# The down projection of a two-layer transformer trunk as seven block products in place of eight, each part right behind its up part

## The chip, the cores and the metric

The kernel runs on one core of a Trainium2 chip. The core has five engines that work side by side and meet by semaphores: TensorE (PE in the rows) multiplies matrices from SBUF into PSUM, VectorE (DVE) and ScalarE (ACT) do elementwise work, GpSimd (POOL) does elementwise work on SBUF alone, and SyncE (SP) issues the DMA transfers. The metric is the device time of one execution in microseconds; lower is better.

## The reference

Two layers, each for a prompt of 512 positions and a sample of 32 (together T = 544 columns, kept feature-major: features on the 128 partitions, positions along the free axis). The changed part is the feed-forward network of a layer:

```
u = rmsnorm(x) @ w_up                       # 1024 -> 2 * 2816
uc = conv_b + causal depthwise conv of width 3 over positions
gate, val = uc[..., :D_FF], uc[..., D_FF:]
f = (jax.nn.gelu(gate, approximate=True) * val) @ w_down      # 2816 -> 1024
x = x + rmsnorm(f, g_post_ffn)
```

Around it stand two attention branches and a per-layer embedding, which the change does not touch.

## The kernel before

**Precision.** A float32 product is made of three passes of a rounded type. Weight and activation are split into a high part (the value rounded) and a low part (value minus high), and `PARTS` runs high*high, high*low, low*high into the same PSUM bank. So each weight chunk needs one rounding and one subtraction (both on POOL), and each activation tile one rounding (ACT) and one subtraction (DVE, helper `lo`, L1099 to L1103).

**Weights.** They come through a ring of four slots in SBUF (`SLOTS`). SP loads chunk after chunk in the order of `STREAM` as soon as TensorE is done with the chunk four places ahead; POOL then rounds it (L616) and writes the low part in place over the loaded values (L623). A chunk is 128 x 1024 (`upg`, `upv` and most `down` chunks), 128 x 768 for the down chunks of the last part.

**The feed-forward part.** Its 2816 hidden features are 22 tiles of 128, in three parts of 8, 8 and 6 tiles (`FFN_PARTS`). An up tile takes two chunks, gate (`upg`) and value (`upv`), each of 8 x 3 x 2 = 48 matmuls of 272 columns. A down chunk `("down", i, j)` multiplies part i's tiles into output tile j of 8: 48 matmuls (36 in the last part), two column halves of 272 in two banks. The order on TensorE is up 0, up 1, down 0, up 2, down 1, down 2, so each down part has another part's work between it and its inputs (`g_s` has two buffers).

**What follows a chunk.** When TensorE is done with an up chunk, DVE scales the result out of PSUM (`u_tile`, L1462 to L1464), ACT starts the convolution (L986 to L995, `conv0`), DVE adds the two other taps (L1470, L1472); after the value chunk DVE multiplies gelu and value into `gt` (L1494, L1495), ACT rounds `gt` (`g_high`, L1007) and DVE makes the low part (`g_low`, through L1101). For the next tile DVE does `u_tile` again first and then the low part. A down result is copied by ACT (down 0, L1023) or added by DVE (down 1 and 2, L1509) into `fT`.

**PSUM.** Banks 4 to 7 hold the convolution; the results of matmuls go in turn into bank pairs (0, 1) and (2, 3). A list of events gives each result tile its banks at build time, and `banks_free` makes TensorE wait until the last user of a bank has been read.

## Time and profile before

| | us |
|---|---|
| median of 3 runs (lowest, highest) | 1851.71 (1851.10, 1852.47) |
| the profiled execution's own time | 1849.15 |
| its span, first to last instruction | 1847.4 |
| TensorE busy | 1824.8 (99%) |
| VectorE busy | 923.5 (50%) |
| ScalarE busy | 559.5 (30%) |
| GpSimd busy | 1075.4 (58%) |

The profile is of one execution. Busy times overlap, since the engines work side by side; their shares say how full an engine is over the whole span and nothing of a single stretch. The profiled execution took 1.75 us more than its span, and the median of the runs is 4.3 us above that span.

### The profile page before, as it was taken

Reading aid. Unit: us, or ns where it says so; the run is one execution under the profiler, and the core shown is the slowest. Engines: PE = TensorE matmul, PEld = TensorE weight load, DVE = VectorE, ACT = ScalarE, POOL = GpSimd, SP = SyncE. Lnnn points to the kernel's source line nnn. Section 1 sums busy time; section 2 is a strip of 40 time slices with the busy share of each in tenths; the row PEclk is TensorE's granted clock in tenths of the full one; section 3 lists DMA queues with packets and bytes.
Section 4 is the critical chain, followed back from the end, with each engine's and each line's share of the span. In section 5 each row is a group of like instructions: output and inputs, shape, how many; then the busy total and the mean of one; then the engine's idle time right before and its main releaser. Section 6 shows DMA issues by size and latency. Waiting matters only on the chain.

```text
span 1847.4 us, 33704 instructions
## 1 busy us (share of the span) xinstructions
PE 1824.8 (99%) x14214; PEld 1768.4 (96%) x14214; DVE 923.5 (50%) x1634; ACT 559.5 (30%) x1197; POOL 1075.4 (58%) x996
## 2 busy tenths in 40 slices
PE   9999999999999999999999999999999999999999
PEld 8999889999999999999999998899999999999999
DVE  6666775232755532523556767752336555235143
ACT  4444443112422211202344445430133222112021
POOL 8686534656555555557665864446456555555564
PEclk9999999999999999999999999999999999999999
DMA  5242112233222222223343421222422222222222
GB/s 189 88 132 86 54 42 84 88 120 112 72 90 92 84 89 92 86 80 97 99 143 93 127 87 47 70 66 84 152 81 75 86 92 89 84 92 91 79 86 95
DMA packets 76231, 170.49 MB, mean 92 GB/s; under 512 B 6384, under 2 KB 34160, under 8 KB 76080
## 3 DMA queue, kind: packets, MB, share of 16 engines
q1 hardware_dynamic: 68752, 160.79, 27.1%
q10 hardware_dynamic: 7328, 7.54, 1.2%
q8 instruction: 113, 1.85, 0.4%
q14 instruction: 38, 0.31, 0.1%
HBM read 156.41 MB, written 9.79 MB: 90 GB/s over the span
## 4 chain that ended last, share of the span: by engine, by line
PE 92%; DVE 5%; ACT 1%; POOL 1%; issue 1%; DMA 0%; SPq 0%; DVEq 0%; ACTq 0%; POOLq 0%
PE ps L1579 76%; PE ps L1614 3%; PE ps L1742 2%; PE ps L1700 2%; DVE xn L1101 1%; DVE xT L1446 1%; DVE mix L1443 1%; PE ps L1796 1%; PE ps L1653 1%; PE ps L1802 1%; DVE R L1101 1%; PE ps L1719 1%; DVE xT L1264 1%; PE ps L1668 1%; PE ps L1738 1%
## 5 line engine op out<-in xcount | busy, mean ns | idle before, releaser
L1579 PE MATMUL ps<-xn,wsp 128*128 128x272 f32 x7824 | 1002.0, 289 | 5.7 <-issue 2.2
L1579 PEld LDWEIGHTS ps<-xn,wsp 128*128 128x128 f32 x7824 | 986.1, 189 | 10.8 <-issue 6.0
L616 POOL CAST wsp<-raw 128x1024 fp32r<-128x1024 f32 (+2 forms) x222 | 220.1, 997 | 505.0 <-DMA raw<-in_wstream 450.3
L623 POOL TENSOR_TENSOR wsp<-raw,wsp 128x1024 fp32r<-128x1024 f32 (+2 forms) x278 | 492.1, 1782 | 16.2
L1579 PE MATMUL ps<-R,wsp 128*128 128x272 f32 x3840 | 486.2, 288 | 0.1
L1579 PEld LDWEIGHTS ps<-R,wsp 128*128 128x128 f32 x3840 | 482.7, 188 | 1.2 <-DVE xT L1130 0.5
L610 POOL TENSOR_TENSOR wsp<-raw,wsp 128x256 fp32r<-128x256 f32 x304 | 235.5, 795 | 12.2
L605 POOL CAST wsp<-raw 128x512 fp32r<-128x512 f32 x152 | 112.2, 738 | 147.9 <-DMA raw<-in_wstream 113.3
L1101 DVE SCALAR_TENSOR_TENSOR R<-ps,R 64x256 fp32r<-64x256 f32 (+12 forms) x264 | 130.0, 510 | 73.2 <-ACT R L753 24.6
L1462 DVE TENSOR_TENSOR mix<-ps,rstd 128x272 f32<-128x272 f32 x88 | 38.8, 441 | 202.9 <-PE ps L1579 192.6
L986 ACT ACTIVATE mix<-vv 128x2 f32<-128x2 f32 x88 | 17.9, 204 | 363.0 <-DVE mix L1464 363.0
L1101 DVE SCALAR_TENSOR_TENSOR R<-mix,R 128x544 fp32r<-128x544 f32 (+2 forms) x86 | 73.2, 852 | 81.1 <-ACT R L1007 66.9
L1470 DVE SCALAR_TENSOR_TENSOR ps<-mix,vv,ps 128x546 f32<-128x546 f32 x88 | 69.4, 789 | 55.6 <-ACT ps L995 55.6
L1614 PE MATMUL ps<-xn,wsp 128*128 128x272 f32 x576 | 80.3, 294 | 6.7 <-DVE xn L1101 6.7
L1614 PEld LDWEIGHTS ps<-xn,wsp 128*128 128x128 f32 x576 | 74.5, 188 | 10.7 <-DVE xn L1101 9.7
L1509 DVE TENSOR_TENSOR A<-ps,A 128x544 f32<-128x544 f32 x32 | 23.2, 724 | 110.1 <-PE ps L1579 110.1
L1264 DVE TENSOR_TENSOR_SCAN xT<-xT 128x128 f32<-128x128 f32 (+3 forms) x64 | 62.9, 1024 | 19.2 <-ACT xT L843 19.2
L995 ACT ACTIVATE ps<-mix,vv 128x546 f32<-128x546 f32 x88 | 71.4, 812 | 1.6 <-DVE mix L1464 1.6
L1472 DVE SCALAR_TENSOR_TENSOR ps<-mix,vv,ps 128x546 f32<-128x546 f32 x88 | 69.6, 791 | 3.1
L1115 DVE TENSOR_TENSOR acc<-acc,mix 128x544 f32<-128x544 f32 x30 | 30.8, 1027 | 64.6 <-ACT mix L666 64.6
L666 ACT ACTIVATE mix<-A 128x544 f32<-128x544 f32 x16 | 10.6, 661 | 150.4 <-DVE A L1509 150.4
L1742 PE MATMUL ps<-R 128*128 128x512 f32 x192 | 52.4, 408 | 0.0
(230 smaller groups left out, 1529.2 us busy)
## 6 DMA issues: line engine op xcount, KB each, us to landing
raw<-in_wstream SPq DMA_DIRECT2D x233, 512.0 KB, 3.5
raw<-in_wstream SPq DMA_DIRECT2D x48, 128.0 KB, 2.6
raw<-in_wstream SPq DMA_DIRECT2D x16, 384.0 KB, 3.0
raw<-in_kc SPq DMA_DIRECT2D x8, 512.0 KB, 3.8
raw<-in_vc SPq DMA_DIRECT2D x8, 512.0 KB, 4.8
xT<-in_x_in SPq DMA_DIRECT2D x8, 272.0 KB, 5.3
out_k_out<-mix ACTq DMA_DIRECT2D x8, 272.0 KB, 2.9
xT<-in_x_in SPq DMA_DIRECT2D x1, 2176.0 KB, 9.2
```

Of the source, the lines that this page charges most:

```text
L605: nc.gpsimd.tensor_copy(dst[:, 0, f], part[:, f]).then_inc(S["w_hi"], 1)
L610: ins = nc.gpsimd.tensor_tensor(dst[:, 1, f], part[:, f], dst[:, 0, f].bitcast(F32), ALU.subtract)
L616: ins = nc.gpsimd.tensor_copy(dst[:, 0, f], part[:, f])
L623: ins = nc.gpsimd.tensor_tensor(dst[:, 1, f], part[:, f], dst[:, 0, f].bitcast(F32), ALU.subtract)
L995: ac(uc[v], e[:, 0:T + 2], ACT.Identity, scale=vv[:, V_CW + f:V_CW + f + 1], bias=vv[:, V_CB + f:V_CB + f + 1]).then_inc(S["conv0"], 1)
L1101: ins = v.scalar_tensor_tensor(dst, src, scale, hi.bitcast(F32), ALU.mult, ALU.subtract)
L1264: v.tensor_tensor_scan(x, x, x, 1.0, ALU.mult, ALU.min).then_inc(S["r_done"], 1)
L1470: link(v.scalar_tensor_tensor(uc[w], uext[w][:, 1:T + 3], vv[:, V_CW + 2 * FT + f:V_CW + 2 * FT + f + 1], uc[w], ALU.mult, ALU.add))
L1472: v.scalar_tensor_tensor(uc[w], uext[w][:, 2:T + 4], vv[:, V_CW + 4 * FT + f:V_CW + 4 * FT + f + 1], uc[w], ALU.mult, ALU.add).then_inc(S[ ...
L1579: mm = pe.matmul(z[:, h], w[:, x, (k0 + k) * P:(k0 + k + 1) * P], rhs[:, y, k, h * HT:(h + 1) * HT], start=(k == 0 and (x, y) == (0, 0)), ...
L1614: mm = pe.matmul(z[:, h], w[:, x, k * P:(k + 1) * P], xn[:, y, k, h * HT:(h + 1) * HT], start=(k == 0 and (x, y) == (0, 0)), stop=(k == KT ...
L1742: mm = pe.matmul(z.rearrange("p r (b q) -> p r b q", b=2), val[:, x, kb], a[:, :, :, kb * P:(kb + 1) * P], start=(kb == 0 and i == 0), sto ...
```

## The change

The eight output tiles of the down projection are taken in pairs (j, j+4), the tiles of a part in two halves of h = 4, 4 and 3, and the 544 columns in two halves of 272 (`HT`). Each pair is then a product of 2 x 2 blocks: weights A11, A12, A21, A22 and activations B11, B12, B21, B22. Strassen's scheme (in Winograd's form) makes it of seven products P1 to P7 of h x 3 matmuls each, on sums of blocks:

- of weights, on DVE (`weight_sum`): S1 = A21 + A22, S2 = S1 - A11, S3 = A11 - A21, S4 = A12 - S2; each is 128 x 512 (384 in the last part) and is rounded by ACT (`sum_high`), its low part made by POOL;
- of activations, on DVE in `product`: T1 to T4 from the halves of `gt`, each 128 x 272, rounded by ACT and split by DVE (`g_low`, `lows_left`);
- of results: P6 goes on top of P1 in its bank and P7 on top of that; ACT copies the bank at each stage into the bank of P2, P3 and P4 (`hand_on`), on which these accumulate; DVE collects into `fT`.

The order is now up 0, down 0, up 1, down 1, up 2, down 2. The sums have one buffer each, so a sum of the next pair waits for the product that reads the present one. The diff, cut to its core:

```diff
-FFN = _up(0) + _up(1) + _down(0) + _up(2) + _down(1) + _down(2)
+    return [("down", i, j + n) for j in range(NP) for n in (0, NP)]
+FFN = _up(0) + _down(0) + _up(1) + _down(1) + _up(2) + _down(2)
+DOWN_LOWS = ("A11", "S1", "S3", "A22", "S2", "A12", "S4")
...
+            if kind == "turn":
+                ring = freed + [4, 5, 6, 7]
+                continue
+            if kind == "lend":
+                BANKS[t] = (ring[0],)
...
+            if c[0] == "down":
+                return ("P2", c[1], c[2]) if c[2] < NP else ("P4", c[1], c[2] - NP)
...
+        DOWN_BY = {"P1": "A11", "P2": "A12", "P3": "S4", "P4": "A22", "P5": "S1", "P6": "S2", "P7": "S3"}
...
@@ gpsimd
+                            if ch[2] < NP:
+                                nc.gpsimd.tensor_copy(dst[:, 0, 0:w], part).then_inc(S["w_hi"], 1)
+                                highs += 1
+                                continue
+                            nc.gpsimd.tensor_copy(hi["A22"], whole_sum["A22"]).then_inc(S["w_hi"], 1)
+                            highs += 1
+                            pool.wait_ge(S["w_hi"], highs)
+                            for n in DOWN_LOWS:
+                                if n in SUMS:
+                                    pool.wait_ge(pre["sum_hi"], sums_made(layer, i, j, n))
+                                pool.wait_ge(pre["sum_raw"], sums_made(layer, i, j, {"A11": "S3", "S1": "S2", "S3": "S3", "A22": "S1"}.get(n, "S4")))
+                                nc.gpsimd.tensor_tensor(lo[n], whole_sum[n], hi[n].bitcast(F32), ALU.subtract).then_inc(S["w_lo"], 1)
...
@@ scalar
+                        for j in range(_F0[i], _F0[i + 1]):
+                            if j == end:
+                                for n in ("S1", "S2", "S3"):
+                                    sum_high(i, 0, n)
+                            u_tile(("upg", j))
+                            if j == end:
+                                sum_high(i, 0, "S4")
+                            u_tile(("upv", j))
+                            if j == end:
+                                hand_on(i, 0, "P1", "P2")
+                            act.wait_ge(S["conv2"], 2 * j + 1)
+                            ac(gel, uc[0], ACT.Gelu_apprx_tanh).then_inc(S["gelu_done"], 1)
+                            g_high(j, (lambda: hand_on(i, 0, "P6", "P3")) if j == end else None)
+                        for j in range(NP):
+                            if j > 0:
+                                hand_on(i, j, "P1", "P2")
+                            if j < NP - 1:
+                                sum_high(i, j + 1, "S1")
+                            if j > 0:
+                                hand_on(i, j, "P6", "P3")
+                            if j < NP - 1:
+                                sum_high(i, j + 1, "S2")
+                                sum_high(i, j + 1, "S3")
+                            hand_on(i, j, "P7", "P4")
+                            if j < NP - 1:
+                                sum_high(i, j + 1, "S4")
...
@@ vector
+                    def product(j):
...
+                        if first:
+                            v.scalar_tensor_tensor(g_raw[:, 1, kk, G_T2], gt[:, HT:T], 1.0, gt[:, 0:HT],
+                                                   ALU.mult, ALU.subtract).then_inc(S["g_raw"], 1)
+                            g_low(j, G_B11, gt[:, 0:HT])
+                            g_low(j, G_T1, g_raw[:, 1, kk, G_T2])
+                            return
+                        v.scalar_tensor_tensor(g_raw[:, 1, kk, G_T4], gt[:, HT:T], 1.0, g_raw[:, 1, kk, G_T2],
+                                               ALU.mult, ALU.subtract).then_inc(S["g_raw"], 1)
+                        g_low(j, G_B21, gt[:, 0:HT])
+                        g_low(j, G_T2, g_raw[:, 1, kk, G_T4])
+                        v.scalar_tensor_tensor(g_raw[:, 1, kk, G_T3], gt[:, HT:T], 1.0, g_raw[:, 1, kk, G_T3],
+                                               ALU.mult, ALU.subtract).then_inc(S["g_raw"], 1)
+                        dve.wait_ge(S["g_lo"], G_LO[j, G_T2])
+                        v.scalar_tensor_tensor(g_raw[:, 1, kk, G_T4], gt[:, 0:HT], 1.0, g_raw[:, 1, kk, G_T4],
+                                               ALU.mult, ALU.subtract).then_inc(S["g_raw"], 1)
...
+                            if j == end:
+                                for n in ("S1", "S2", "S3"):
+                                    weight_sum(i, 0, n)
+                            if j != 1:
+                                u_tile(("upg", j))
+                            if j == end:
+                                weight_sum(i, 0, "S4")
+                            if j > _F0[i]:
+                                lows_left(j - 1, (G_B22, G_T3))
+                            taps(("upg", j))
+                            u_tile(("upv", j))
...
+                            if j > _F0[i]:
+                                lows_left(j - 1, (G_T4,))
+                            taps(("upv", j))
+                            product(j)
+                        lows_left(end, (G_B22, G_T3, G_T4))
+                        for j in range(NP):
...
+                            collect(i, "P5", j, ((j + NP, 1), (j, 1)), True)
+                            if j < NP - 1:
+                                for n in ("S1", "S2", "S3"):
+                                    weight_sum(i, j + 1, n)
+                            dve.wait_ge(S["dve_read"], dread(("P5", i, j)))
+                            collect(i, "P2", j, ((j, 0),), True)
...
@@ tensor
+                        for j in range(NP):
+                            down_product("P1", i, j)
+                            down_product("P5", i, j)
+                            if j == 0:
+                                down_product("P6", i, j, range(h - 1))
+                                down_product("P2", i, j, range(h - 1))
+                                down_product("P6", i, j, range(h - 1, h))
+                                down_product("P2", i, j, range(h - 1, h))
+                            else:
+                                down_product("P6", i, j)
+                                down_product("P2", i, j)
+                            down_product("P7", i, j)
+                            down_product("P3", i, j)
+                            down_product("P4", i, j)
```

How this moves the instructions, at three places.

DVE, before: the last up tile of a part in layer 0 (its gate chunk's `u_tile` first; L1101 is a low part, L1509 the next down results).

```order
L1462 TENSOR_TENSOR mix<-ps,rstd 128x272 [waits tail_done_0,conv2_0,p_done_0]
L1463 TENSOR_TENSOR mix<-ps,rstd 128x240
L1464 TENSOR_TENSOR mix<-ps,rstd 128x32
L1101 SCALAR_TENSOR_TENSOR R<-mix,R 128x544 [waits g_hi_0]
...
L1494 TENSOR_TENSOR mix<-mix,ps 128x512 [waits conv2_0,gelu_done_0]
L1495 TENSOR_TENSOR mix<-mix,ps 128x32
L1101 SCALAR_TENSOR_TENSOR R<-mix,R 128x544 [waits g_hi_0]
L1509 TENSOR_TENSOR A<-ps,A 128x544 [waits p_done_0,act_read_0] x8
```

DVE, now: the last up tile of a part in layer 0 (L1660 are the weight sums S1, S2, S3 and, further down, S4; L1236 low parts; L1627, L1631, L1634 the sums T of activations; L1597 opens `u_tile`).

```order
L1660 SCALAR_TENSOR_TENSOR RF<-raw 128x512 [waits p_done_0,raw_in0,raw_in3]
L1660 SCALAR_TENSOR_TENSOR RF<-RF,raw 128x512 [waits sum_raw,p_done_0]
L1660 SCALAR_TENSOR_TENSOR raw<-raw 128x512
L1597 TENSOR_TENSOR mix<-ps,rstd 128x272 [waits tail_done_0,conv2_0,p_done_0]
...
L1660 SCALAR_TENSOR_TENSOR ukF<-raw,RF 128x512 [waits sum_raw,p_done_0]
L1236 SCALAR_TENSOR_TENSOR R<-mix,R 128x272 [waits g_hi_0]
L1236 SCALAR_TENSOR_TENSOR R<-RF,R 128x272 [waits g_hi_0]
...
L1627 SCALAR_TENSOR_TENSOR RF<-mix,RF 128x272 [waits g_raw_0]
L1236 SCALAR_TENSOR_TENSOR R<-mix,R 128x272 [waits g_hi_0]
L1236 SCALAR_TENSOR_TENSOR R<-RF,R 128x272 [waits g_hi_0]
L1631 SCALAR_TENSOR_TENSOR RF<-mix,RF 128x272
```

Three weight sums have come ahead of the gate chunk's `u_tile`, a fourth sum and two low parts ahead of its taps, and one low part of 544 columns has become sums and low parts of 272.

POOL, before: two down chunks (a rounding and a subtraction each, both waiting only for the load and for the rounding).

```order
L616 CAST wsp<-raw 128x1024 [waits raw_in0]
L623 TENSOR_TENSOR wsp<-raw,wsp 128x1024 [waits w_hi_0]
L616 CAST wsp<-raw 128x1024 [waits raw_in1]
L623 TENSOR_TENSOR wsp<-raw,wsp 128x1024 [waits w_hi_0]
L616 CAST wsp<-raw 128x1024 [waits raw_in2]
```

POOL, now: the two down chunks of one pair (j, j+4).

```order
L684 CAST wsp<-raw 128x1024 [waits raw_in3]
L687 CAST wsp<-raw 128x512 [waits raw_in0]
L694 TENSOR_TENSOR wsp<-raw,wsp 128x512 [waits sum_raw,w_hi_0]
L694 TENSOR_TENSOR R<-RF,R 128x512 [waits sum_raw,sum_hi]
L694 TENSOR_TENSOR wsp<-raw,wsp 128x512 [waits sum_raw,sum_hi]
L694 TENSOR_TENSOR wsp<-raw,wsp 128x512 [waits sum_raw]
L694 TENSOR_TENSOR R<-RF,R 128x512 [waits sum_raw,sum_hi]
L694 TENSOR_TENSOR wsp<-raw,wsp 128x512 [waits sum_raw]
L694 TENSOR_TENSOR ukT<-ukF,ukT 128x512 [waits sum_raw,sum_hi]
```

Two subtractions of 1024 columns have become seven of 512, each of which waits for DVE's weight sums (`sum_raw`), and those of S1 to S4 for ACT's rounding too (`sum_hi`).

## Rows read from the trace of the kernel before

**Rows 1.** The page, parts 1 and 2: TensorE's line and its granted clock

```profile
PE 1824.8 (99%) x14214; PEld 1768.4 (96%) x14214; DVE 923.5 (50%) x1634; ACT 559.5 (30%) x1197; POOL 1075.4 (58%) x996
PEclk9999999999999999999999999999999999999999
```

**Rows 2.** Waits of TensorE (waited for: us in total, times, longest us)

```profile
PE ps L1614 <- DVE xn L1101: 6.7, 12, 1.6
```

**Rows 3.** TensorE in order of time (start us, us, engine line op), layer 0

```profile
482.07 180.77 PE L1579 MATMUL ps<-xn,wsp 128*128 128x272 f32 x1440
662.68 48.27 PE L1579 MATMUL ps<-R,wsp 128*128 128x272 f32 x384
782.95 85.84 PE L1579 MATMUL ps<-R,wsp 128*128 128x272 f32 x684
```

**Rows 4.** All engines in order of time, one up tile and the next

```profile
765.11 0.44 DVE L1462 TENSOR_TENSOR mix<-ps,rstd 128x272 f32<-128x272 f32 x1 [1.54 <-PE ps L1579]
...
765.78 0.18 DVE L1464 TENSOR_TENSOR mix<-ps,rstd 128x32 f32<-128x32 f32 x1
...
768.71 1.04 POOL L616 CAST wsp<-raw 128x1024 fp32r<-128x1024 f32 x1 [2.59 <-DMA raw<-in_wstream]
...
769.82 2.39 POOL L623 TENSOR_TENSOR wsp<-raw,wsp 128x1024 fp32r<-128x1024 f32 x1
771.12 0.44 DVE L1462 TENSOR_TENSOR mix<-ps,rstd 128x272 f32<-128x272 f32 x1 [1.21 <-PE ps L1579]
...
773.09 0.79 DVE L1470 SCALAR_TENSOR_TENSOR ps<-mix,vv,ps 128x546 f32<-128x546 f32 x1 [1.12 <-ACT ps L995]
...
775.41 0.18 DVE L1495 TENSOR_TENSOR mix<-mix,ps 128x32 f32<-128x32 f32 x1
775.60 2.40 POOL L623 TENSOR_TENSOR wsp<-raw,wsp 128x1024 fp32r<-128x1024 f32 x1
777.13 0.44 DVE L1462 TENSOR_TENSOR mix<-ps,rstd 128x272 f32<-128x272 f32 x1 [1.54 <-PE ps L1579]
```

**Rows 5.** The same view where a low part on DVE meets POOL

```profile
503.92 1.04 POOL L616 CAST wsp<-raw 128x1024 fp32r<-128x1024 f32 x1 [2.52 <-DMA raw<-in_wstream]
...
504.43 1.10 DVE L1101 SCALAR_TENSOR_TENSOR R<-mix,R 128x544 fp32r<-128x544 f32 x1 [1.70 <-ACT R L1007]
505.04 2.76 POOL L623 TENSOR_TENSOR wsp<-raw,wsp 128x1024 fp32r<-128x1024 f32 x1
...
787.71 2.39 POOL L623 TENSOR_TENSOR wsp<-raw,wsp 128x1024 fp32r<-128x1024 f32 x1
788.35 2.33 DVE L1101 SCALAR_TENSOR_TENSOR R<-mix,R 128x544 fp32r<-128x544 f32 x1 [0.73 <-ACT R L1007]
```

**Rows 6.** POOL's groups by shape (busy us, mean ns of one)

```profile
L623 POOL TENSOR_TENSOR wsp<-raw,wsp 128x1024 fp32r<-128x1024 f32 x166 | 401.4, 2418 | 13.3
L623 POOL TENSOR_TENSOR wsp<-raw,wsp 128x768 fp32r<-128x768 f32 x8 | 14.7, 1842 | 0.6
L616 POOL CAST wsp<-raw 128x768 fp32r<-128x768 f32 x16 | 13.2, 824 | 35.6 <-DMA raw<-in_wstream 35.5
L623 POOL TENSOR_TENSOR R<-raw,R 128x256 fp32r<-128x256 f32 x16 | 11.3, 734 | 0.5
L616 POOL CAST R<-raw 128x512 fp32r<-128x512 f32 x8 | 4.8, 610 | 0.0
```

**Rows 7.** DVE's groups by shape

```profile
L1101 DVE SCALAR_TENSOR_TENSOR R<-ps,R 128x512 fp32r<-128x512 f32 x48 | 30.9, 678 | 2.4 <-ACT R L774 1.3 <-ACT R L885 0.5 <-ACT vtail L741 0.4
L1462 DVE TENSOR_TENSOR mix<-ps,rstd 128x272 f32<-128x272 f32 x88 | 38.8, 441 | 202.9 <-PE ps L1579 192.6 <-ACT rstd L659 10.3
```

**Rows 8.** ACT's copies of 256 columns out of PSUM (ns, min/median/max)

```profile
L794 ACT ACTIVATE acc<-ps x4: 383/383/383, 128.7 to 1116.1; 128x256 f32<-128x256 f32 x4
```

**Rows 9.** The page, part 6: weight loads, us from issue to landing

```profile
raw<-in_wstream SPq DMA_DIRECT2D x233, 512.0 KB, 3.5
raw<-in_wstream SPq DMA_DIRECT2D x16, 384.0 KB, 3.0
```

More of the change, by code:

```diff
@@ L35 @@
 FFN_PARTS = [8, 8, 6]
+NP = KT // 2
 SLOTS = 4
@@ L82, in ring_slot, with lows @@
     return (layer * NST + ST_AT[c]) % SLOTS
+DOWN_LOWS = ("A11", "S1", "S3", "A22", "S2", "A12", "S4")
+def lows(c):
+    return sum((len(DOWN_LOWS) if m[2] >= NP else 0) if m[0] == "down" else 1 for m in STREAM[:ST_AT[c] + 1])
 def chunk_floats(c):
@@ L361, in build @@
             EVENTS.append(("done", t))
-        whole(("nm", 2), *FFN[2:], ("plep", 4), ("nm", 3), ("plep", 5), ("plep", 6), ("plep", 7))
+        whole(("nm", 2))
+        for i in range(len(FFN_PARTS)):
+            whole(*_up(i)[2 if i == 0 else 0:])
+            EVENTS.append(("turn", None))
+            for j in range(NP):
+                EVENTS += [("lend", ("P7", i, j)), ("done", ("P1", i, j)), ("lend", ("P5", i, j)), ("done", ("P5", i, j)),
+                           ("lend", ("P2", i, j)), ("done", ("P6", i, j)), ("lend", ("P3", i, j)), ("done", ("P2", i, j)),
+                           ("lend", ("P4", i, j)), ("done", ("P7", i, j)), ("done", ("P3", i, j)), ("done", ("P4", i, j))]
+        whole(("plep", 4), ("nm", 3), ("plep", 5), ("plep", 6), ("plep", 7))
         for j in range(3):
@@ new lines, in sum_high, with hand_on @@
+                    def sum_high(i, j, n):
+                        if (i, j) != (0, 0):
+                            act.wait_ge(S["p_done"], AT[({"S1": "P5", "S2": "P6", "S3": "P7", "S4": "P3"}[n], *pair_before(i, j))] + 1)
+                        act.wait_ge(pre["sum_raw"], sums_made(layer, i, j, n))
+                        ac(down_parts(layer, i, j, 0)[n], down_sums(layer, i, j)[n], ACT.Copy).then_inc(pre["sum_hi"], 1)
+                    def hand_on(i, j, n, to):
+                        act.wait_ge(S["dve_read"], max(dread(o) for o in BEFORE[(to, i, j)]))
+                        act.wait_ge(S["p_done"], AT[(n, i, j)] + 1)
+                        ac(bank((to, i, j))[:, 0:HT], bank(("P7", i, j))[:, 0:HT], ACT.Copy).then_inc(S["act_read"], 1)
@@ new lines, in g_low, with lows_left, weight_sum @@
+                    def g_low(j, n, src):
+                        kk = g_place(j)[2]
+                        dve.wait_ge(S["g_hi"], G_HI[j, n])
+                        lo(g_s[:, 1, kk, n], src, g_s[:, 0, kk, n], "g_lo")
+                    def lows_left(j, names):
+                        if not g_place(j)[3]:
+                            for n in names:
+                                g_low(j, n, gt[:, HT:T] if n == G_B22 else g_raw[:, 1, g_place(j)[2], n])
+                    def weight_sum(i, j, n):
+                        if n == "S1":
+                            for m in (j, j + NP):
+                                dve.wait_ge(raw_in[ring_slot(layer, ("down", i, m))], 16 * LOADS[layer * NST + ST_AT[("down", i, m)]])
+                        if (i, j) != (0, 0) and n != "S3":
+                            dve.wait_ge(S["p_done"], AT[({"S1": "P5", "S2": "P6", "S4": "P3"}[n], *pair_before(i, j))] + 1)
+                        if n in ("S2", "S4"):
+                            dve.wait_ge(pre["sum_raw"], sums_made(layer, i, j, "S1" if n == "S2" else "S3"))
+                        a = down_sums(layer, i, j)
+                        x, y = {"S1": ("A21", "A22"), "S2": ("S1", "A11"), "S3": ("A11", "A21"), "S4": ("A12", "S2")}[n]
+                        v.scalar_tensor_tensor(a[n], a[x], 1.0, a[y], ALU.mult, ALU.add if n == "S1" else ALU.subtract).then_inc(pre["sum_raw"], 1)
@@ new lines, in collect @@
+                    def collect(i, n, j, places, new):
+                        t = (n, i, j)
+                        dve.wait_ge(S["p_done"], AT[t] + 1)
+                        if n == "P7":
+                            dve.wait_ge(S["act_read"], aread(t))
+                        for m, h in places:
+                            f, z = fT[:, m, h * HT:(h + 1) * HT], bank(t)[:, 0:HT]
+                            if i == 0 and new:
+                                ins = v.tensor_copy(f, z)
+                            else:
+                                ins = v.tensor_tensor(f, z, f, ALU.add)
+                        ins.then_inc(S["dve_read"], 1)
```

242 lines of the change are left out of this document (149 added, 93 removed).

## The prediction

> **What bounds the kernel now.** I read the page's busy times and granted clock first, then TensorE's waits, then its stretches in order of time, then all engines over one up tile. TensorE is busy 1824.8 of 1847.4 us at a granted clock of full speed in every slice (2.4 GHz, the upper level) [rows 1]; its longest single wait is 1.6 us and lies at a norm [rows 2]. In the feed-forward network there is none: 1440 matmuls run in 180.77 us without a gap, and a down part of 384 in 48.27 us [rows 3], 125.7 ns each. So time is won only by fewer matmuls, and lost by anything that makes TensorE wait here, where it never waits now.
>
> **What is removed.** Before, a layer's down projection has 22 x 8 x 3 x 2 = 1056 matmuls, now 7 x (4 + 4 + 3) x 3 x 4 = 924, of the same 272 columns. Over two layers 264 go: 264 x 0.1257 = 33.2 us, all of it on the path [rows 3].
>
> **What the rest of the work must keep up with.** A product is 12 matmuls, 1.51 us (9 and 1.13 us in the last part); a pair is 10.56 us (7.92). An up chunk takes 6.02 us: DVE's `u_tile` comes at 765.11, 771.12 and 777.13 [rows 4].
>
> The price is in the second inputs of DVE. An instruction on DVE with both inputs in SBUF and one on POOL do not overlap. The low part at 788.35 takes 2.33 us: POOL's subtraction ends at 790.10, and DVE ends 0.58 us behind it. The one at 504.43 ends 0.57 us behind POOL's rounding (504.96), and then POOL's subtraction at 505.04 takes 2.76 us, not 2.39, since it waits for DVE [rows 5]. So each waits for the other's whole instruction, and they take turns. Before, DVE has one such instruction per up tile, placed where POOL idles (767.6, POOL starts at 768.71 [rows 4]). Now a first-half tile has three of 272 columns, a second-half tile eight; a pair has four weight sums of 512. `u_tile`, the taps, gelu times value and the collecting read PSUM and one SBUF input and stay out of it. I take 0.44 us for one of 272 columns and 0.70 for one of 512 [rows 7].
>
> POOL's subtraction: 734 ns for 256 columns, 1842 for 768, 2.39 us for 1024 [rows 4, 6], a straight line that gives 1.29 us for 512 and 1.01 for 384; back to back 1.26 and 0.98. A pair costs POOL 1.04 + 0.61 of rounding (0.82 + 0.50) and 7 x 1.26 = 8.8 (6.9): 10.5 us without one turn for DVE, of TensorE's 10.56. Four turns of about 0.6 make it 12.9.
>
> **Step 1: DVE falls behind in the second half of the up part.** The value `gt` is ready at 775.59, and POOL's subtraction starts at 775.60 and runs to 778.0 [rows 4]: the two low parts and the two further sums behind it start only then, five instructions of 0.44 in all, to 780.1. The next `u_tile` was due at 777.13: 3.0 us late. The leftovers of that tile (B22, T3, T4) then stand before POOL's next rounding and subtraction, and so each tile ends somewhat later: by the same bookkeeping 3.0, 3.7, then 4 to 5 us. TensorE doesn't wait yet (it can bear 6.0 with its two bank pairs). I take 4.3 at the last tile (3.7 in the last part, with two second-half tiles before the last).
>
> **Step 2: the join from up to down.** Zero is TensorE's end of the part's last value chunk. Three weight sums (2.2 us) stand ahead of the last gate chunk's `u_tile` on DVE; they end at -6.02 + 4.3 + 2.2 = +0.5. Behind them are queued that `u_tile`, the taps, all of the last tile, and every POOL subtraction of pair 0, since A11 waits for S3. POOL from there: A11 at 1.85, S1 3.65, S3 5.15, A22 6.65, S2 7.9, A12 9.15, S4 10.65, with DVE's turns between. DVE: `u_tile` to 1.4; S4 2.45; B22 3.95; T3 5.45; taps 7.1; `u_tile` 8.0; T4 9.45; taps 11.1; `gt` 12.0 (before: 4.5 us from the end of the chunk to `gt` [rows 4]); T2's sum, low B21 and low T2 to X = 13.55. TensorE has 42 matmuls (5.3 us) that it can do before the last tile's T2 is there, and idles the rest: 1.85 for P1, 0.3 for P5, 2.75 for P6, 0.1 for P2 and 3.25 for the last tile, 8.3 us in all. In the last part, by the same steps with 1.01 for POOL, X = 11.1 against 30 matmuls (3.8): 7.3 us. Sum: 4 x 8.3 + 2 x 7.3 = 47.8 us. Bounds: if DVE met POOL nowhere, X would be 6.7 and the stall 1.4 (the last tile's chain alone); if it also lost the race for every slot, about 12.
>
> **Step 3: pair 0 to pair 1.** ACT hands P7's bank to P4 only behind the roundings of pair 1's S1, S2, S3, whose sums DVE begins only when low T4 is done: S3 at X + 5.1, rounding 0.6, copy 0.4 (256 columns take 383 ns [rows 8]): P4 could start at X + 3.9 and starts at X + 6.2. 2.4 us x 6 = 14.4. Between 0 and 3.
>
> **Step 4: pairs 1 to 3.** The loop that decides: POOL's first five subtractions to S2 (6.3 + one turn 0.6), P6 (1.5), DVE's S2 and S3 of the next pair, each behind a POOL instruction (2.9), the rounding of A22 (0.7): 12.0 to 12.9 us against 10.56. The loads (3.5 us behind P2 and P4 [rows 9]) are just inside it. Followed pair by pair, TensorE waits 1.25, 2.75 and 1.6 us at P6: 5.6 x 4 = 22.4; in the last part 1.0, 2.0, 2.2, 10.4 for both layers. Sum 32.8. Bounds: 0 if DVE's sums hit only POOL's idle time, 50 if each turn costs a whole subtraction.
>
> **Edits at nothing.** ACT's extra roundings and copies (some 4 us per pair of 10.56) lie under TensorE; the next part's first up chunks are ready before P4 of pair 3 ends; the collecting (six adds of 0.44 per pair) fits DVE. What hides them is idle time of ACT and DVE, and where it is gone steps 2 to 4 have counted it.
>
> **Sum.** 1847.4 - 33.2 + 47.8 + 14.4 + 32.8 = 1909.2 us of span. The profiled execution ran 1.75 us longer than its span and the median is 4.3 above the span, so I predict 1912.
>
> Of POOL's price the Trainium skill says something else (GPSIMD Engine Reference, "Performance versus the Vector engine"): about 2.6 cycles an element at 1.2 GHz for two inputs. By that estimate 512 columns take 1.11 us, and the seven of a pair would be 1.2 us cheaper, which would nearly empty step 4's waits and give some 1890; the rows of this case (734, 1842 and 2418 ns) contradict it, and I go by them.
>
> **Rivals.**
> A. *POOL and DVE fit* (faster). They take turns so that DVE's clusters fall into POOL's idle 2.5 us per up chunk [rows 4], and down pairs run at TensorE's pace. Left are 1.4 us per join and little else: 1851.7 - 33.2 + 9 = 1828, up to 1845 with a wait of a us or two per pair. For it: POOL is at 58% and DVE at 50% over the whole [rows 1]. Against: shares over the span; in the down pairs the sum for POOL is 10.5 of 10.56 before any turn, and `gt` is ready at the very moment when POOL starts.
> B. *Half* (slower or near nothing). The lag of step 1 doesn't grow over 2 us, and the pairs lose one turn, not two: joins of 6 us, step 3 of 1, pairs 1 to 3 of 1 each: 36 + 6 + 18 = 60, less 33: 1851.7 + 27 = 1879; its own range 1852 to 1890.
> C. *The clock falls* (slower still). TensorE idles up to 3.3 us at once in step 2, twice in 8 us, with a us or two of work between. No row of before shows so long a gap, and the granted clock is full throughout [rows 1, 2]. If it drops to 1.2 GHz at each join, the 4 us of matmuls between and behind the gaps take 8: 6 x 4 more, 1936; if at pairs too, 1960. The Trainium skill states that an idle TensorE falls back to half rate (TensorE: Matmul & The Clock Gate, "Part 1: The HAM clock gate (the "warmup" mystery)"); no run here shows it yet, and by it this case is likelier than I make it.
>
> **Chances.** The forecast 0.56 (its own range 1885 to 1930), A 0.17, B 0.17, C 0.10. The time is the forecast's. The range of 8 in 10 reaches from the upper end of A into C: 1842 to 1940. A change within 0.2% is about what a measurement of this kernel can't tell from none: 1848 to 1855.4 has 0.04, from the edges of A and B; faster 0.15; slower 0.81.
>
> **What would show it.** In the new trace: 13,950 matmuls; gaps of TensorE of 1 to 4 us at the first pair's P5, P6 and P2 of each of six parts, 8 us in all, ended by POOL's and DVE's low parts; DVE's `u_tile` 3 to 5 us late in tiles 5 to 7; DVE's sums of 272 and 512 columns with means well over 0.44 and 0.70; POOL near 100% in down parts; waits at P6 for the low part of S2. I am wrong if TensorE's down parts run at 42 us without gaps (A), if the waits at the join end with DVE but measure under 5 us (B), or if the sums' means are not lengthened, for then the turns aren't what costs.

## The result, and the profile after

The changed kernel takes **1894.64 us** (median of 4 runs, 1893.33 to 1896.2); the kernel before took 1851.4 beside it. The ratio is 1.0235, with a 95% interval of 1.0217 to 1.0253: it is 2.4% slower. The forecast was 1912, with a range of 1842 to 1940. The profiled execution ran 1893.98 us, with a span of 1892.2.

The page's first line and TensorE's groups for the new products (busy us, mean ns of one, then idle before), where [rows 1] stood:

```profile
PE 1817.7 (96%) x13950; PEld 1751.2 (93%) x13950; DVE 1185.2 (63%) x2040; ACT 669.9 (35%) x1481; POOL 1189.5 (63%) x1100
...
L2191 PE MATMUL ps<-R,wsp 128*128 128x272 f32 x1056 | 153.8, 301 | 5.4 <-issue 5.3
...
L2191 PE MATMUL ps<-R 128*128 128x272 f32 x528 | 80.2, 299 | 41.1 <-POOL R L694 19.5
```

264 matmuls are gone, as announced. In exchange TensorE now waits in the down parts, 46.5 us by these two groups, and some of its matmuls ran slow (means of 299 to 301 ns, against 289 for the others). Its waits (us in total, times, longest), where [rows 2] had 6.7 us at the norms as the largest:

```profile
PE ps L2191 <- POOL R L694: 19.5, 16, 1.9
PE ps L2191 <- issue: 16.5, 14, 3.1
PE ps L1820 <- DVE xn L1236: 10.6, 12, 2.0
PE ps L2191 <- DVE R L1236: 6.3, 4, 1.9
PE ps L2191 <- POOL wsp L694: 3.5, 2, 1.8
```

TensorE in order of time over the first down part's pair 0 and the first two pairs behind it, where [rows 3] had one unbroken row:

```profile
566.69 1.66 PE L2191 MATMUL ps<-R,wsp 128*128 128x272 f32 x12
568.19 1.67 PE L2191 MATMUL ps<-R 128*128 128x272 f32 x12
572.51 2.38 PE L2191 MATMUL ps<-R 128*128 128x272 f32 x9 [2.65 <-issue]
574.68 1.81 PE L2191 MATMUL ps<-R,wsp 128*128 128x272 f32 x9
576.34 0.62 PE L2191 MATMUL ps<-R 128*128 128x272 f32 x3
...
577.53 1.74 PE L2191 MATMUL ps<-R,wsp 128*128 128x272 f32 x12 [0.21 <-issue]
579.11 1.68 PE L2191 MATMUL ps<-R,ukT 128*128 128x272 f32 x12
582.39 3.26 PE L2191 MATMUL ps<-R,wsp 128*128 128x272 f32 x24 [1.61 <-issue]
585.49 1.67 PE L2191 MATMUL ps<-R 128*128 128x272 f32 x12
588.17 1.78 PE L2191 MATMUL ps<-R 128*128 128x272 f32 x12 [1.01 <-POOL R L694]
...
600.38 1.77 PE L2191 MATMUL ps<-R 128*128 128x272 f32 x12 [1.18 <-POOL R L694]
```

P1 and P5 run with no wait. P6 waits 2.65 us. Its first 9 matmuls then take 2.17 us from their start to that of the next row, where 9 take 1.13 us at full speed; the granted clock over 572.6 to 574.4 is 0.50. The wait of 1.61 stands before P4. From there a pair takes 12.2 us (588.17 to 600.38), with one wait at P6, for GpSimd (the low part of S2).

These times give an account of each down part. The nominal time of a pair is 84 matmuls of 0.1257, 10.56 us (63 and 7.92 in the last part). Pair 0's excess is the start of P1 of pair 1, less the start of P1 of pair 0, less that. The rest of the part's excess is that of pairs 1 to 3. The sums are good to some 0.3 us, since a few starts lie inside a merged row. Over the six parts:

| | pair 0, us | pairs 1 to 3, us |
|---|---|---|
| forecast | 62.2 (steps 2 and 3) | 32.8 (step 4) |
| measured | 40.9 (6.7, 7.4, 6.7, 6.7, 6.9, 6.5) | 32.2 (4.6, 4.9, 6.8, 4.6, 4.6, 6.8) |

1847.4 - 33.2 + 40.9 + 32.2 = 1887.3. Of the 4.9 us left to the span of 1892.2, 3.9 are the norms' longer waits (10.6 against 6.7).

Why a pair takes 12.2 us is seen in the busy times of one pair (window; then us, and the busy us of PE, PEld, DVE, ACT and POOL, each with its count; then clock, DMA share, GB/s):

```profile
588.17:600.38 12.21, 11.03 (x84) 10.66 (x84) 7.87 (x11) 3.58 (x7) 12.13 (x10) 1.00 0.28 87
```

GpSimd is busy for 12.13 of 12.21 us (an instruction that waits for its turn counts as busy): it is the bound. GpSimd's and VectorE's groups by shape show what the turns do to single instructions; they answer to [rows 6, 7]:

```profile
L694 POOL TENSOR_TENSOR wsp<-raw,wsp 128x512 fp32r<-128x512 f32 x64 | 93.1, 1465 | 45.4 <-DVE raw L1660 44.8
L694 POOL TENSOR_TENSOR R<-RF,R 128x512 fp32r<-128x512 f32 x32 | 42.6, 1332 | 0.0
...
L1236 DVE SCALAR_TENSOR_TENSOR R<-mix,R 128x272 fp32r<-128x272 f32 x66 | 80.6, 1222 | 6.9 <-ACT RF L1102 6.5
L1660 DVE SCALAR_TENSOR_TENSOR ukF<-raw,RF 128x512 f32<-128x512 f32 x16 | 24.2, 1513 | 0.0
L1660 DVE SCALAR_TENSOR_TENSOR RF<-RF,raw 128x512 f32<-128x512 f32 x16 | 18.5, 1159 | 11.2 <-PE ps L2191 10.6
```

A sum of 512 columns that meets nobody takes 0.69 us; here the means are 1.16 and 1.51. A low part of 272 columns takes 0.44 alone; the group shown has a mean of 1.22, and the other group of such low parts (88 of them) one of 0.64.

### The profile page after: what moved, and what is told of

It is laid out like the page before. It is cut to its first block, busy times and chain, and to the rows that moved or that the text cites. A ratio compares the mean times of both kernels' runs of the same rounds, so it can differ in the third digit from the quotient of the medians.

```text
span 1892.2 us, 34472 instructions
## 1 busy us (share of the span) xinstructions
PE 1817.7 (96%) x13950; PEld 1751.2 (93%) x13950; DVE 1185.2 (63%) x2040; ACT 669.9 (35%) x1481; POOL 1189.5 (63%) x1100
## 4 chain that ended last, share of the span: by engine, by line
PE 69%; DVE 16%; POOL 7%; issue 4%; ACT 3%; DMA 0%; SPq 0%; DVEq 0%; POOLq 0%; ACTq 0%
PE ps L1785 51%; DVE R L1236 4%; PE ps L2191 3%; POOL wsp L694 3%; PE ps L1820 2%; PE ps L1948 2%; POOL R L694 2%; PE ps L1906 2%; DVE ps L1605 1%; DVE xn L1236 1%; DVE xT L1581 1%; DVE mix L1578 1%; DVE ps L1607 1%; ACT ps L1091 1%; DVE RF L1627 1%
## 5 line engine op out<-in xcount | busy, mean ns | idle before, releaser
L719 POOL TENSOR_TENSOR wsp<-raw,wsp 128x1024 fp32r<-128x1024 f32 (+1 forms) x214 | 388.5, 1827 | 12.4
L712 POOL CAST wsp<-raw 128x1024 fp32r<-128x1024 f32 (+1 forms) x174 | 174.0, 1007 | 332.5 <-DMA raw<-in_wstream 280.3
L706 POOL TENSOR_TENSOR wsp<-raw,wsp 128x256 fp32r<-128x256 f32 x304 | 242.9, 820 | 12.2
L1785 PE MATMUL ps<-R,wsp 128*128 128x272 f32 x1728 | 221.5, 289 | 1.3 <-DVE A L1673 1.2
L1785 PEld LDWEIGHTS ps<-R,wsp 128*128 128x128 f32 x1728 | 218.0, 189 | 2.9 <-issue 1.6
L1236 DVE SCALAR_TENSOR_TENSOR R<-ps,R 64x256 fp32r<-64x256 f32 (+12 forms) x264 | 129.8, 510 | 71.9 <-ACT R L849 23.8
L694 POOL TENSOR_TENSOR wsp<-raw,wsp 128x512 fp32r<-128x512 f32 (+1 forms) x96 | 131.1, 1376 | 69.3 <-DVE raw L1660 68.3
L2191 PE MATMUL ps<-R,wsp 128*128 128x272 f32 x1056 | 153.8, 301 | 5.4 <-issue 5.3
L2191 PEld LDWEIGHTS ps<-R,wsp 128*128 128x128 f32 x1056 | 144.3, 198 | 9.6 <-issue 7.7
L1236 DVE SCALAR_TENSOR_TENSOR R<-mix,R 128x272 fp32r<-128x272 f32 (+3 forms) x108 | 107.6, 996 | 21.1 <-ACT R L1046 11.6
L2191 PE MATMUL ps<-R 128*128 128x272 f32 x528 | 80.2, 299 | 41.1 <-POOL R L694 19.5
L2191 PEld LDWEIGHTS ps<-R 128*128 128x128 f32 x528 | 71.2, 193 | 47.3 <-POOL R L694 23.9
L1605 DVE SCALAR_TENSOR_TENSOR ps<-mix,vv,ps 128x546 f32<-128x546 f32 x88 | 69.5, 789 | 70.6 <-ACT ps L1091 70.4
L1820 PE MATMUL ps<-xn,wsp 128*128 128x272 f32 x576 | 80.2, 295 | 10.6 <-DVE xn L1236 10.6
L1820 PEld LDWEIGHTS ps<-xn,wsp 128*128 128x128 f32 x576 | 74.5, 188 | 14.7 <-DVE xn L1236 13.6
L1673 DVE TENSOR_TENSOR A<-ps,A 128x272 f32<-128x272 f32 x112 | 46.7, 436 | 51.4 <-PE ps L2191 32.4
```

The source lines that it names most:

```text
L694: nc.gpsimd.tensor_tensor(lo[n], whole_sum[n], hi[n].bitcast(F32), ALU.subtract).then_inc(S["w_lo"], 1)
L706: ins = nc.gpsimd.tensor_tensor(dst[:, 1, f], part[:, f], dst[:, 0, f].bitcast(F32), ALU.subtract)
L712: ins = nc.gpsimd.tensor_copy(dst[:, 0, f], part[:, f])
L719: ins = nc.gpsimd.tensor_tensor(dst[:, 1, f], part[:, f], dst[:, 0, f].bitcast(F32), ALU.subtract)
L1236: ins = v.scalar_tensor_tensor(dst, src, scale, hi.bitcast(F32), ALU.mult, ALU.subtract)
L1605: link(v.scalar_tensor_tensor(uc[w], uext[w][:, 1:T + 3], vv[:, V_CW + 2 * FT + f:V_CW + 2 * FT + f + 1], uc[w], ALU.mult, ALU.add))
```

## The experiments

Eleven kernels were run: five made from the changed kernel and two made from the kernel before tell the causes apart, two measure the clock's price, and two try to mend the loss.

**Order alone.** The kernel before, with the parts in the changed kernel's order and nothing else:

```
-FFN = _up(0) + _up(1) + _down(0) + _up(2) + _down(1) + _down(2)
+FFN = _up(0) + _down(0) + _up(1) + _down(1) + _up(2) + _down(2)
```

> The kernel before with one thing changed: the order up 0, down 0, up 1, down 1, up 2, down 2, with the plain eight block products (no sums, no Strassen). If putting a down part right behind its up part costs by itself: the last tile's low part is ready some 7.7 us after TensorE's last value chunk, TensorE has 42 matmuls (5.3 us) without it, in the last part 30 (3.8 us), so it waits 2.4 us four times and 3.9 twice: 17 us more than before, about 1868. If the loss is all in the sums and subtractions of the scheme: within 3 us of before, 1851 to 1854.

Measured: 1871.57 us, ratio 1.0111 (1.0095 to 1.0128). So 20.2 us of the 43 are the new order's and 23.1 the scheme's, which removes 33.2 us of matmuls and so costs some 56. (The scheme in the old order was not run, so this split holds for the order first and the scheme on top of it.) The place, in this kernel's all-engine view:

```profile
571.24 2.35 POOL L623 TENSOR_TENSOR wsp<-raw,wsp 128x1024 fp32r<-128x1024 f32 x1
571.65 2.51 DVE L1101 SCALAR_TENSOR_TENSOR R<-mix,R 128x544 fp32r<-128x544 f32 x1 [0.73 <-ACT R L1007]
574.22 5.96 PEld L1579 LDWEIGHTS ps<-R,wsp 128*128 128x128 f32 x35 [2.77 <-DVE R L1101]
574.22 6.06 PE L1579 MATMUL ps<-R,wsp 128*128 128x272 f32 x34 [2.56 <-DVE R L1101]
```

Even here the last tile's low part stands behind a GpSimd subtraction, and TensorE, which before had a whole up part to do in between, waits for it: 14.2 us in six waits, all of 2.3 to 2.6. Behind the wait its matmuls ran at a granted clock of 0.59 over 574 to 578, where full speed is 1.00. So it was at four of the six joins (0.57 to 0.60 over the 4 us behind the wait); at the second join of each layer the clock stayed at 1.00.

**The same order, GpSimd's subtractions without reads** (the low parts of the up and down weights are zeros):

```
-    tensor_tensor(low, part, high, subtract)
+    memset(low, 0); memset(low, 0)          # two writes of 1 us each
```

> The kernel before with the new order of parts alone; in it the low parts of the up and down weights are written by GpSimd as zeros, in two writes of some 1 us each, and read nothing (the low parts of these products are left out of the computation). At the turn from up to down VectorE's last low part of an activation took 2.51 us behind GpSimd's subtraction of 2.35 us, against 0.73 us where GpSimd was idle, and TensorE waited 2.56 us for it. If the turns of the two engines cause that, 1.8 us of each of the six waits go: 1871.6 - 6 x 1.8 = 1861, and 1857 if TensorE then keeps its clock. If the wait is VectorE's own chain of work, it stays at 1870 to 1872.

Measured: 1863.42 us in one run. The same place:

```profile
571.28 1.96 POOL L618 MEMSET wsp<- 128x1024 f32 x2
571.94 0.73 DVE L1108 SCALAR_TENSOR_TENSOR R<-mix,R 128x544 fp32r<-128x544 f32 x1 [0.73 <-ACT R L1014]
572.72 1.52 PE L1586 MATMUL ps<-R,wsp 128*128 128x272 f32 x10 [0.77 <-DVE R L1108]
```

VectorE's low part runs in 0.73 us inside GpSimd's writes, and 1.8 of the 2.56 us go, as expected. The six waits fell together from 14.2 to 8.5 us, and the longest is still 2.8, so the whole gave back 8.2 us, not 10.6.

**The down parts' low parts as one short write** (low parts of the down weights are zeros):

```
-    tensor_tensor(lo[n], whole_sum[n], hi[n], subtract)
+    memset(lo[n], 0)
```

> The changed kernel, but POOL's seven subtractions per pair are each one memset of the same 512 columns, which reads nothing and is short (the low parts of the down weights are left out of the result). POOL keeps its place in every wait. If POOL's work and its turns with DVE are what costs: waits at P6 in pairs 1 to 3 go, DVE's weight sums take 0.69 us each, only the chain of the last tile is left at each join (1 to 2 us): span 1835 to 1850. If the chain of single buffers and hand-overs is what costs (S1 behind P5, S2 behind P6, the copies on ACT): the span stays within 15 us of 1892.

**The same with two writes each.**

> The changed kernel, but each of POOL's subtractions is two memsets of 512 columns one after the other, about as long as the subtraction (1.1 to 1.3 us) but without reading SBUF (the low parts of the down weights are left out of the result). It parts POOL's length from its turns with DVE. If the turns cost (each engine waits for the other's instruction): DVE's weight sums are back at 0.69 us, a pair costs POOL 10.5 us, just TensorE's 10.56, and the span is 1855 to 1868. If POOL's own length is what costs: 1880 to 1892, with DVE's sums short.

Measured in one run each: 1851.89 and 1854.47 us, with spans of 1850.1 (1835 to 1850 expected) and 1852.7 (under the 1855 to 1868 expected). So GpSimd's length by itself hardly matters (2.6 us, and four runs of one kernel lie up to 4.6 us apart here), while two writes that read nothing in place of a subtraction that reads give back 40 us. By the account above pairs 1 to 3 fell from 32.2 to 4.7 us and pair 0 from 40.9 to 27.6. One caution: two writes take 1.05 us and an undisturbed subtraction 1.28, so this kernel is a little short of the same length. In the next run GpSimd keeps its full length.

**VectorE's weight sums without reads** (the four sums of a pair are zeros; the text below says ten, and it is four):

```
-    scalar_tensor_tensor(a[n], a[x], 1.0, a[y], mult, add or subtract)
+    memset(a[n], 0)
```

> VectorE's ten sums of down weights per pair are memsets, which read nothing (so the down products are wrong in their numbers; all else stands), while GpSimd keeps its seven subtractions. If the loss comes from instructions of VectorE with two inputs in SBUF and GpSimd's taking turns, most of what the seven empty low parts gave back (39.5 us) comes back here too: 1855 to 1870. If it is GpSimd's chain of seven subtractions by itself (their number and order), it stays at 1885 to 1895.

Measured: 1867.06 us in one run, 27.6 us less, in the range that the turns give; pairs 1 to 3 cost 11.6 us and pair 0 33.2. Here it is VectorE that is a little short: its write of 512 columns takes 0.49 us, an undisturbed sum 0.69. The busy times of one pair with the other partner silenced; here and in the next two fences the columns are those of the window above. First this kernel, then the two writes:

```profile
588.18:598.73 10.55, 10.55 (x87) 10.55 (x85) 4.47 (x10) 2.95 (x6) 10.47 (x10) 1.00 0.31 100
```

```profile
591.08:601.64 10.56, 10.56 (x87) 10.56 (x86) 6.00 (x11) 3.48 (x7) 9.49 (x17) 1.00 0.31 99
```

GpSimd keeps all its work, subtractions included, and needs 10.47 us of a pair's 10.55; with the reading sums present the same work takes 12.13. The 1.66 us of difference is the price of VectorE's four sums per pair, and there was 0.08 us of room for it (1.07 with the two writes). With either partner silenced the pairs of the long parts run at TensorE's pace from pair 2 on at the latest, and this settles step 4.

**No reads in the up parts either** (low parts of the up weights zeros too):

> As the run with low parts made by two writes each and no reads (1854.5 us), and in addition GpSimd's subtractions for the up chunks are two writes of the same tile and no reads (so the low parts of up and down weights are zeros; the rest of the computation stands). If VectorE's delay in the second half of an up part comes from taking turns with those subtractions, it is gone, and the turns from up to down cost 1 to 3 us each in place of 3 to 5: 1835 to 1845. If that delay is VectorE's own work on the new sums of activations, the time stays at 1850 to 1855.

Measured: 1851.24 us in one run, 3.2 us under the one run with two writes, which is within the spread of one kernel's runs; the rival held. Pair 0 costs 25.7 us over the six parts, where it cost 27.6. So what VectorE loses to the up parts' subtractions costs little at the join. TensorE's rows in pair 0 show what is left when GpSimd's subtractions read nothing:

```profile
572.46 0.65 PE L2201 MATMUL ps<-R 128*128 128x272 f32 x3 [1.26 <-DVE R L1246]
...
578.55 3.27 PE L2201 MATMUL ps<-R,wsp 128*128 128x272 f32 x24 [1.61 <-issue]
```

That is a wait of 1.26 us for the last tile (the prediction's lower bound was 1.4) and the 1.61 us before P4 as in the changed kernel. The new order and ScalarE's order take these without any turn of GpSimd's subtractions.

**Step 3 by itself.** ScalarE hands P7's bank to P4 before it rounds pair 1's sums:

```
+    if j == 0: hand_on(i, j, "P7", "P4"); sum_high(i, j + 1, "S1")
     sum_high(i, j + 1, "S2"); sum_high(i, j + 1, "S3")
-    hand_on(i, j, "P7", "P4")
```

> The full computation, with one thing moved: in pair 0 of each down part ScalarE copies P7's bank for P4 right when P7 is done, ahead of the high parts of S1, S2 and S3 of pair 1. That is step 3 of the prediction by itself, forecast there at 2.4 us at 6 places and seen in the changed kernel as a wait of 1.6 us before P4 at the four longer parts and 0.3 to 0.5 us at the two shorter. If this wait is one that TensorE really has on its path: 4 x 1.6 + 2 x 0.4 = 7 us less than the changed kernel's 1894.6, so 1886 to 1889. The rival is that GpSimd's chain of subtractions sets when pair 1 can run, and that pair 0 only waits somewhat earlier for it: then the wait moves to P6 of pair 1, and the time stays at 1893 to 1896.

Measured: 1895.61 us, ratio 1.0246 (1.0229 to 1.0263): nothing gained; the rival held. (The changed kernel has the wait of 1.6 us before P4 in the two long parts of layer 0, not in four as that text says; in the long parts of layer 1 there is none, and in the last parts it is 0.3 and 0.5.) The wait before P4 is gone, and more is waited at P6 of pair 1, for GpSimd:

```profile
581.94 3.19 PE L2195 MATMUL ps<-R,wsp 128*128 128x272 f32 x24
584.97 1.67 PE L2195 MATMUL ps<-R 128*128 128x272 f32 x12
588.00 1.78 PE L2195 MATMUL ps<-R 128*128 128x272 f32 x12 [1.37 <-POOL R L694]
```

Over the six parts pair 0 fell from 40.9 to 36.1 and pairs 1 to 3 rose from 32.2 to 37.5. P6 of pair 1 starts 21.6 us behind the part's first matmul, where it started 21.5 behind it: GpSimd's chain from the sums of pair 1 sets that time, and what TensorE does before only decides where it waits.

**The clock's price, in the changed kernel.** Matmuls of no use fill the gaps of pair 0:

```
+    for _ in range(24): matmul(columns nobody reads)    # before P6; 16 in the last part
+    8 before the last tile's part of P6, 10 before P4
-    VectorE copies P5 of pair 0 when P5 is done
+    VectorE copies P5 of pair 0 when P6 is done    # the fills write in P5's bank
```

The fills do not leave the down results intact, so this kernel is of use for its times alone.

> The changed kernel with matmuls that have no use put where TensorE waits in pair 0 of each part: 24 (16 in the last part) before P6, 8 before the last tile's part of P6, 10 before P4, into unused columns of P5's bank. If the fall of the granted clock to 0.5 behind the gap costs time by itself: the clock stays at 1.00 at the joins and the time falls by 6 to 10 us, to some 1886. If the slower matmuls only fill time that TensorE would wait anyway, or the clock is not held by it: 1892 to 1900.

Measured: 1895.54 us, ratio 1.024 (1.0225 to 1.0255), with a mean clock of 0.998 in place of 0.993. The clock was kept and the time was not gained: P6's first 9 matmuls took 1.36 us in place of 2.38, and pair 0 cost 40.3 us in place of 40.9. The later copy of P5 is not what ate the gain, since VectorE starts it 11.9 us behind the part's first matmul here and 11.8 in the changed kernel.

**The clock's price, in the kernel with the order alone:**

```
+    if k == nk - 1: for _ in range(20): matmul(columns nobody reads)
```

> The kernel before with the new order of parts alone, plus 20 matmuls of no use in front of the last matmuls of the last up tile that each down part waits with (into columns of the bank that nobody reads; the result is unchanged). With the order alone the time was 1871.6 us, and at the turn from up to down TensorE idled 2.3 to 2.6 us and then ran about 3 us at a lower granted clock. If that lower clock costs time there, keeping TensorE busy through the wait gives back about 1.6 us at each of 6 turns: 1862. If, as in the changed kernel, the slower matmuls only fill time in which TensorE would wait further on, the time stays at 1871 to 1873.

Measured: 1867.35 us, ratio 1.009 (1.0075 to 1.0105), 4.2 us less than without, where 9 was expected; the two intervals overlap, so the size is loose. The row of the same join:

```profile
572.79 2.23 PE L1577 MATMUL ps<-masks 128*128 128x240 bf16 x20
575.60 4.66 PE L1583 MATMUL ps<-R,wsp 128*128 128x272 f32 x35 [0.59 <-DVE R L1101]
```

The granted clock stayed 1.00 over 574 to 578, and this down part took 51.03 us against 52.45. The same holds join by join: at the four joins where the clock had fallen the down part is shorter by 1.4 to 1.6 us, and at the two where it had not it is 0.3 to 0.4 longer. The expectation had counted on six. The slower clock costs where TensorE's own work sets the end (here), and nothing where another engine's chain does.

**VectorE makes the sums' low parts.** GpSimd is left with three subtractions a pair:

```
-DOWN_LOWS = ("A11", "S1", "S3", "A22", "S2", "A12", "S4")
+DOWN_LOWS = ("A11", "A22", "A12")     # S1 to S4: on VectorE, behind each sum
```

> The full computation. The low parts of S1 to S4 are made by VectorE itself, right behind their sums, and GpSimd makes only those of A11, A22 and A12; so GpSimd has three instructions per pair in place of seven, and the two engines take turns less often. My theory (the wait at P6 is for the low part of S2, which GpSimd ends late because its seven subtractions and VectorE's sums take turns): the wait of 1.0 to 1.2 us at P6 and the 1.6 us at P4 of pair 0 go, about 18 pairs by 1.6 us and 6 parts by 1 to 2, in all 30 to 40 us: 1850 to 1865. The rival (VectorE's own chain of sums, evictions and roundings sets the pace, and four more of its instructions make it longer): 1880 or more, with the waits put down to VectorE in place of GpSimd.

Measured: 1888.18 us, ratio 1.02 (1.0183 to 1.0217): 6.5 us less, far from the 30 to 40 expected and in the rival's band. Half of the theory held. From pair 2 on, the pairs of the long parts run near TensorE's pace:

```profile
598.23:608.84 10.61, 10.61 (x87) 10.61 (x85) 9.14 (x15) 3.40 (x7) 6.62 (x6) 1.00 0.32 100
```

Pairs 1 to 3 cost 16.3 us in place of 32.2, but pair 0 rose from 40.9 to 52.1. At the join VectorE is the late one, as the rival said, and the low parts given to it make it later: P6 of pair 0 waits 3.74 us in the first part and 20.1 over the six, each time for a low part on VectorE.

**The split version:** pair 0's low parts on GpSimd, those of pairs 1 to 3 as in the run before, and the hand-over first:

```
+DOWN_LOWS = {0: ("A11", "S1", "S3", "A22", "S2", "A12", "S4"), 1: ("A11", "A22", "A12")}
```

> The full computation: as the run with the hand-over first, and in pairs 1 to 3 VectorE makes the low parts of the four sums, while pair 0's are left to GpSimd. GpSimd's instructions per pair took 12.5 us in the changed kernel, more than the 10.56 us of TensorE's matmuls, and with three of its seven subtractions it is no longer the bound: the pairs ran at 10.6 us when VectorE made all of them, and only the turn from up to down got worse. So, by my theory, each of the four longer down parts takes 42.2 + 5 us in place of 53.8 and the two shorter save some 5 us: 1894.6 - 26 - 10 = 1859 (1855 to 1868). If the gain of the pairs is given back at the turn there (VectorE late with the next sums), 1875 to 1888.

Measured: 1877.38 us, ratio 1.0147 (1.0132 to 1.0162). This is 17.3 us better than the changed kernel, and half of what was expected: pair 0 costs 36.0 us and pairs 1 to 3 21.0. The time is in the rival's band, but not for its reason, since pair 0 costs what it did with the hand-over first (36.1). What stays: TensorE now waits for ScalarE's hand-over (12.3 us in 14 waits, up to 2.1 in pair 1), and pairs 1 to 3 of a last part cost 6.3 us together. It doesn't beat the kernel before, and no run points to a version that does.

## Why the prediction was right in its direction and high by 17 us

The bound named in the prediction was found: an instruction of VectorE with two inputs in SBUF and a reading one of GpSimd do not overlap. It is shown from both sides, by silencing either partner (one run each, but 40 and 28 us, far above the spread of a kernel's runs).

**The removal** (33.2 us) was right: 13,950 matmuls, and 10.55 us for a pair where nothing waits.

**Step 4** was right in mechanism: a loop of 12.0 to 12.9 forecast and 12.2 measured, the wait at P6 for the low part of S2, GpSimd full. That the sum came out so well, 32.8 forecast and 32.2 measured, is in part luck: the four long parts cost 18.7 us where 22.4 were forecast, and the two last parts 13.6 where 10.4 were. The single waits were 1.0 to 1.3 us in the long parts, more even than the 1.25, 2.75 and 1.6 of the text, and the four sums cost GpSimd 1.66 us a pair, 0.4 each where the text had 0.6. The other price that the prediction names for GpSimd, 1.11 us for 512 columns, came near in time with its "some 1890", but not by its reason: undisturbed, the subtraction took 1.27 to 1.29 us.

**Step 1 is the step that was mis-sized.** It put VectorE 4.3 us late at the last tile (3.7 in a last part). In the first part its gate chunks' `u_tile` was late by 2.7 us at both of the tiles where the text had 3.0 and 3.7, so the lag did not grow, and at the last tile the first weight sum began 1.0 us late (1.0 to 1.4 in the four long parts, 0.6 to 0.7 in the last parts). The all-engine view of the changed kernel there:

```profile
559.86 0.44 DVE L1627 SCALAR_TENSOR_TENSOR RF<-mix,RF 128x272 f32<-128x272 f32 x1
...
561.51 0.43 DVE L1634 SCALAR_TENSOR_TENSOR RF<-mix,RF 128x272 f32<-128x272 f32 x1
...
561.87 0.69 DVE L1660 SCALAR_TENSOR_TENSOR RF<-raw 128x512 f32<-128x512 f32 x1
...
563.20 0.68 DVE L1660 SCALAR_TENSOR_TENSOR raw<-raw 128x512 f32<-128x512 f32 x1
...
564.02 1.29 POOL L694 TENSOR_TENSOR wsp<-raw,wsp 128x512 fp32r<-128x512 f32 x1 [4.97 <-DVE raw L1660]
```

VectorE's sums of activations and the three weight sums run undisturbed at 0.44 and 0.69 us each, because GpSimd idles for 4.97 us before 564.02. The chunks in its stream at this place are the down weights of pair 0, which it only rounds; their subtractions wait for S3. The prediction gave these slots the up parts' subtraction of 2.39 us. S3's sum ended at 563.88, 2.7 us before TensorE's end of the up part at 566.6 (2.4 to 2.8 before the down part's first matmul in the long parts, 3.5 in the last); the forecast was 0.5 behind it.

**Step 2** inherits that. From S3 on, the chain to the last tile's low T2 took 12.4 us (to 576.25), against 13.05 forecast; it simply began 3.2 us earlier. So X was 9.6, not 13.55, P1 and P5 had no wait, and TensorE's waits up to the last tile's products were 2.9 to 4.3 us in the six parts (2.69, 1.30 and 0.20 in the join of layer 1 below), not 8.3. One of the prediction's own signs of being wrong was that the join's waits end with VectorE but measure under 5 us (rival B); the size came true, and the releaser in part, since the first wait ends with another engine. The first of the waits is 2.65 to 3.07 us in the long parts; put down to "issue", it ends in the first part with ScalarE's hand-over of P1's bank (572.06 to 572.41), which stands behind that engine's part of the last `u_tile`; S2's low part, for which the text had P6 wait, had been ready at 571.14. In the two last parts the first wait (1.8 and 1.7 us) does end with a low part on GpSimd.

**Step 3** was seen, 1.6 us in two parts and 0.3 and 0.5 in two others where 2.4 was forecast in each of six, but it did not stand in the sum in its own right. It and step 4 were added as if they followed each other; moving the hand-over shows that they are one wait for one GpSimd chain, put in two places. With 14.4 us for step 3 and 47.8 for step 2, against 40.9 in pair 0 together, the forecast was 21.3 us high here, and the 4.9 us outside the down parts were missed; the second error hides part of the first.

**Rival B** came nearest in time, 1879. It had the joins and step 3 right (36 + 6 = 42 us against 40.9; the lag of step 1 didn't grow, though it was 2.7 us and not under 2) and the pairs too low (18 against 32.2); its joins with the forecast's step 4 would have given 1889 of span. **Rival A** failed as its own counter-argument said: shares of the whole span, 58% and 50% [rows 1], don't show a stage in which GpSimd has 0.08 us of room. **Rival C's** event took place and its cost did not. A join of layer 1:

```profile
1512.66 1.36 PE L2191 MATMUL ps<-R 128*128 128x272 f32 x9 [2.69 <-issue]
...
1516.46 0.64 PE L2191 MATMUL ps<-R 128*128 128x272 f32 x3 [1.30 <-DVE R L1236]
...
1517.67 2.85 PE L2191 MATMUL ps<-R,wsp 128*128 128x272 f32 x12 [0.20 <-issue]
1520.33 2.14 PE L2191 MATMUL ps<-R,ukT 128*128 128x272 f32 x12
1522.54 3.27 PE L2191 MATMUL ps<-R,wsp 128*128 128x272 f32 x24
```

and the granted clock in two windows of it:

```profile
1514.00:1518.00 4.00, 2.50 (x18) 2.08 (x17) 3.44 (x9) 1.99 (x6) 1.76 (x2) 0.99 0.00 0
1518.00:1522.00 4.00, 4.00 (x22) 4.00 (x21) 3.68 (x8) 1.94 (x4) 0.42 (x1) 0.58 0.43 133
```

P7 and P3 run at half speed here, and P4 then comes without its 1.6 us wait. Pair 0's excess is 6.7 us in both layers, whether as a wait or as slow matmuls.

## What to carry to other kernels

Before moving work onto two engines that take turns, add up one period of the tightest stage for each, alone and then with every meeting; here a stage with 0.1 us of room in 10.5 had none. Reordering work so that a consumer follows its producer at once has a price of its own, so time it alone first: here it was 20 of the 43 us lost. Waits behind one slow chain don't add (moving one of them gained nothing here); before summing two of them, ask whether the second would still be there with the first removed.
